# When GpSimd multiplies in a routing head: products tied to VectorE's three lists, and the low parts of down tiles moved behind them

## The reference

```
q = (xt @ w_query).reshape(T, 8, 2, 128)                     # 8 retrieval heads, 2 halves
s = einsum('thpd,hpnd->thpn', q, sub_keys)                   # 128 keys per half
top_s, top_i = top_k(s, 16)                                  # two lists of 16 per head
cand = top_s[:, :, 0, :, None] + top_s[:, :, 1, None, :]
best_s, best_c = top_k(cand, 16)                             # third list
i1, i2 = take_along_axis(top_i[..0], best_c // 16), take_along_axis(top_i[..1], best_c % 16)
ids = i1 * 128 + i2;  gates = softmax(best_s)
a = einsum('tkd,td->tk', expert_down[ids], x)                # 128 experts of 16384 per token
y = einsum('tk,tkd->td', gelu(a) * gates, expert_up[ids])
```

## Time and profile before

| what | us |
|---|---|
| median of three runs | 1589.13 |
| the profiled execution, and its span | 1590.72, 1588.6 |
| head 0 of routing (264.84 to 309.93) | 45.09 |
| heads 1 to 6 (309.93 to 532.80) | 222.87 |
| head 7 and tail (532.80 to 600) | 67.2 |
| TensorE busy over the span | 1487.9 (94%) |
| VectorE, ScalarE, GpSimd busy | 1198.0, 624.7, 591.5 |
| granted TensorE clock, mean | 0.986 |

### The profile page before, as it was taken

The page is one execution under the profiler, slowest core; times in us unless marked ns, Lnnn a source line. Parts: engine busy times, 40 slices in busy tenths (PEclk is TensorE's granted clock), DMA queues, the critical chain, the costliest instruction groups (busy, mean ns, idle before and its releaser), DMA issues.

```text
span 1588.6 us, 21566 instructions
## 1 busy us (share of the span) xinstructions
PE 1487.9 (94%) x7670; PEld 1280.3 (81%) x7670; DVE 1198.0 (75%) x2406; ACT 624.7 (39%) x984; POOL 591.5 (37%) x459
## 2 busy tenths in 40 slices
PE   3999997999999889999968999999999999999997
PEld 3575545998888779999967888888888888888886
DVE  6546435778999987888815887887877887888887
ACT  1114324343344446667713333333343333333333
POOL 0000011225555436999921333334424343443340
PEclk9999998999999999999989999999999999999999
DMA  9962300446444345899987999999989999999993
GB/s 332 361 227 107 107 26 15 144 158 212 158 163 158 118 141 189 243 259 275 283 252 261 343 338 352 350 337 355 341 313 358 346 348 364 339 345 365 342 326 145
DMA packets 258442, 404.90 MB, mean 255 GB/s; under 512 B 120664, under 2 KB 175520, under 8 KB 258208
## 3 DMA queue, kind: packets, MB, share of 16 engines
q1 hardware_dynamic: 122496, 243.87, 43.7%
q0 software_dynamic: 36864, 134.23, 23.5%
q10 hardware_dynamic: 98976, 25.43, 6.9%
HBM read 360.49 MB, written 42.99 MB: 254 GB/s over the span
## 4 chain that ended last, share of the span: by engine, by line
PE 56%; DVE 13%; POOL 5%; issue 5%; ACT 2%; DMA 1%; ACTq 1%; SPq 0%; POOLq 0%; DVEq 0%
PE bank L1695 10%; PE bank L1696 10%; PE bank L1697 10%; PE bank L1639 7%; PE bank L1641 7%; PE bank L1640 7%; POOL gated L672 4%; PE bank L1677 2%; DVE dlo L1204 2%; DVE cand L1248 2%; DMA down<-in_down_t 1%; DVE topi L1194 1%; DVE top L1191 1%; ACTq L916 1%; DVE pick L1232 1%
## 5 line engine op out<-in xcount | busy, mean ns | idle before, releaser
L1639 PE MATMUL bank<-h2hi,dhi 128*128 128x384 f32 x1024 | 351.8, 344 | 45.5 <-DVE dlo L1204 44.2
L1641 PE MATMUL bank<-h2hi,dlo 128*128 128x384 f32 x1024 | 346.3, 338 | 0.0
L1640 PE MATMUL bank<-h2lo,dhi 128*128 128x384 f32 x1024 | 346.0, 338 | 0.0
L1204 DVE TENSOR_TENSOR dlo<-down,dhi 128x1024 fp32r<-128x1024 f32 x128 | 168.0, 1314 | 191.2 <-ACT dhi L820 191.1
L1695 PE MATMUL bank<-uhi,ahi 128*128 128x512 f32 x768 | 300.0, 391 | 4.6 <-DVE ulo L1373 4.6
L1696 PE MATMUL bank<-ulo,ahi 128*128 128x512 f32 x768 | 300.0, 391 | 0.0
L1697 PE MATMUL bank<-uhi,alo 128*128 128x512 f32 x768 | 299.6, 390 | 0.0
L639 POOL DMA_INDIRECT rows<-in_peer_down,ids x128 | 155.3, 1213 | 266.8 <-DVE rows L1217 223.0
L639 POOL DMA_INDIRECT rows<-in_peer_up,ids x128 | 159.6, 1246 | 246.2 <-DVE y L1226 221.3
L1639 PEld LDWEIGHTS bank<-h2hi,dhi 128*128 128x128 f32 x1024 | 194.9, 190 | 54.8 <-DVE dlo L1204 50.7
L1640 PEld LDWEIGHTS bank<-h2lo,dhi 128*128 128x128 f32 x1024 | 195.2, 191 | 2.7
(11 more groups left out here) (198 smaller groups left out, 2030.6 us busy)
## 6 DMA issues: line engine op xcount, KB each, us to landing
down<-in_down_t SPq DMA_DIRECT2D x128, 512.0 KB
up<-in_peer_up SPq DMA_DIRECT2D x128, 512.0 KB
ada<-in_w_ada SPq DMA_DIRECT2D x12, 2048.0 KB, 16.2
gate<-gates_dram SPq DMA_DIRECT2D x128, 192.0 KB
gates_dram<-stage ACTq DMA_DIRECT2D x5, 4096.0 KB, 28.8
gel_dram<-gel SPq DMA_DIRECT2D x80, 192.0 KB
gelu<-gel_dram SPq DMA_DIRECT2D x80, 192.0 KB
wq<-in_peer_query SPq DMA_DIRECT2D x16, 512.0 KB, 4.6
```

The lines of the kernel that those rows point to most:

```text
L1204: ve.tensor_tensor(dlo[s][:], down[s][:], dhi[s][:].bitcast(F32), ALU.subtract).then_inc(dve_dlo, 1)
L1639: pe.matmul(bank[7 * s][:, 0:TD], dhi[s][:, k, :], h2hi[:, k, 0:TD], start=k == 0, stop=False)
L1640: pe.matmul(bank[7 * s][:, 0:TD], dhi[s][:, k, :], h2lo[:, k, 0:TD], start=False, stop=False)
L1641: last = pe.matmul(bank[7 * s][:, 0:TD], dlo[s][:, k, :], h2hi[:, k, 0:TD], start=False, stop=k == KT - 1)
```

## The change

GpSimd's work in a head gets a new order and new waits. For head h (1 to 7) it now waits, by the count of low parts (`dve_dlo`), until VectorE stands at the start of the first list of head h. There it makes `split_wq(h+1, 0)` and the first multiplication of `weigh_hits(h-2)`. It waits until VectorE is past the low part behind the first list, and makes the second multiplication and `split_wq(h+1, 1)`. It waits until the sums of head h are written (`dve_half`), and makes `measure_hits(h-1)`. The gathers come after that.

VectorE's low parts leave the middle of the lists (but for the last head) and stand behind each list. The one ahead of the sums moves ahead of `select`. A fifth stands behind the dots, and head 0 makes one more, so that VectorE is one tile further ahead at the start of each head. The dots in heads fall from 15 to 12 (heads 3 to 6, none in head 7), and `DOTS_ROUTING` from 18 to 15, so the last 3 dots are taken in the main stage.

```diff
-DOTS_ROUTING = DOTS_HEAD * (PH - FIRST_DOTS) + DOTS_PICKS
+DOTS_ROUTING = DOTS_HEAD * (PH - 1 - FIRST_DOTS) + DOTS_PICKS
+def lows_by_head(h):
+    return IN_FRONT + 1 + PER_HEAD * (h + 1)
 # GpSimd
     def measure_hits(h):
+                if h + 2 < PH:
+                    gp.wait_ge(dve_half, h + 2)
...
-            def weigh_hits(h):
+            def weigh_hits(h, s):
+                gp.wait_ge(act_hit, 2 * h + s + 1)
                 gp.wait_ge(dve_top, h + 1)
...
-            for h in range(PH):
-                if h >= FIRST_DOTS - 1:
-                    gathers(min(DOTS_HEAD * (h + 1 - FIRST_DOTS) + ROWS_KEPT + ROWS_HEADS, DOTS_ROUTING))
-                measure_hits(h)
-                weigh_hits(h)
+            for h in range(1, PH):
+                for s in range(2):
+                    if s == 0 or h + 1 < PH:
+                        gp.wait_ge(dve_dlo, lows_by_head(h - 1) + s)
+                    if h + 1 < PH and s == 0:
+                        split_wq(h + 1, 0)
+                    if h >= 2:
+                        weigh_hits(h - 2, s)
+                    if h + 1 < PH and s == 1:
+                        split_wq(h + 1, 1)
+                measure_hits(h - 1)
+                if h >= 2:
+                    gathers(min(DOTS_HEAD * max(h - FIRST_DOTS, 0) + ROWS_KEPT + ROWS_HEADS, DOTS_ROUTING))
+            for s in range(2):
+                weigh_hits(PH - 2, s)
+            measure_hits(PH - 1)
+            gathers(DOTS_ROUTING)
+            for s in range(2):
+                weigh_hits(PH - 1, s)
             gathers(DOTS_ROUTING + ROWS_KEPT)
 # VectorE
-                    top16(lambda b: score[s][:, b, :], lambda b: top[:, s, b, :], lambda b: topi[:, s, b, :], next_lo)
-                    if last:
-                        next_lo()
+                    top16(lambda b: score[s][:, b, :], lambda b: top[:, s, b, :], lambda b: topi[:, s, b, :],
+                          next_lo if last and s else no_lo)
+                    next_lo()
                     if h >= 2 and s == 1 - last:
                         select(h - 2)
                         expert_numbers(h - 2)
-                if last:
-                    sums(h, next_lo)
-                else:
-                    next_lo()
-                    sums(h, lambda: None)
+                sums(h, next_lo if last else no_lo)
...
                 picks_of(h)
-                next_lo()
-                if h >= FIRST_DOTS:
+                if not last:
+                    next_lo()
+                if FIRST_DOTS <= h < PH - 1:
                     for n in range(DOTS_HEAD * (h - FIRST_DOTS), DOTS_HEAD * (h + 1 - FIRST_DOTS)):
                         row_op(n)
+                next_lo()
+                if h == 0:
+                    next_lo()
```

More of the change, by code:

```diff
@@ L643, in _ @@
                     split_wq(h, s)
-            split_wq(2, 0)
             asked = 0
@@ L1204, in down_lo, with no_lo @@
                 ve.tensor_tensor(dlo[s][:], down[s][:], dhi[s][:].bitcast(F32), ALU.subtract).then_inc(dve_dlo, 1)
-            lows = iter(range(FIRST_G))
+            next_low = 0
             def next_lo():
-                n = next(lows)
-                down_lo(n, n % 2)
+                nonlocal next_low
+                down_lo(next_low, next_low % 2)
+                next_low += 1
+            def no_lo():
+                pass
             def row_op(n):
@@ L1340, in _ @@
                 next_lo()
-            assert next(lows, None) is None
+            assert next_low == FIRST_G
             down_lo(FIRST_G, 0)
```

14 lines of the change are left out of this document (5 added, 9 removed).

## The result

| what | before | after | change | forecast |
|---|---|---|---|---|
| median (us) | 1587.44, four runs | 1560.93 (1559.59 to 1561.73), four runs | ratio 0.9833, interval 0.9808 to 0.9859 | 1569, range 1561 to 1583 |
| profiled execution, its span | 1590.72, 1588.6 | 1561.73, 1559.9 | -29.0, -28.7 | 1570.7 |
| head 1 (between first MAX8s) | 34.37 | 33.80 | -0.57 | 0 |
| heads 2 to 6 | 188.50 | 170.65 | -17.85 | -16.6 |
| head 7 and tail, to the first gate product | 77.5 | 72.5 | -5.0 | -3.4 |

The start and the end of the program give the other 0.4. The kernel became faster by 1.7%, where the forecast was 1.3%.

The account below looks back on a forecast made before the run. VectorE, slowed 9.1 us a head by operations colliding with GpSimd products, was taken to hold heads 2 to 6 above TensorE's floor; 1590.7 - 16.6 (heads) - 3.4 (tail) = 1570.7 profiled, so 1569 us median, range 1561 to 1583.

Parts of the forecast that it names:

- The premise: Heads: VectorE's list operations are free beside GpSimd products; MAX8 takes 0.66 and 0.86 against 0.87 us with none running.
- the sum of 9.1 us a head: Head 4, VectorE: cast, sums, low part and list's cast lengthened beside GpSimd products by 1.70 + 3.96 + 1.28 + 2.18.
- Heads 2 to 6: Routing heads: TensorE becomes the bound and each head falls to head 1's 34.37 us, a gain of 16.6 us.
- the other end of the bound: Heads 2 to 6: the floor of head 1's busy time, 34.08 us a head, a gain of 18.1 us.
- The tail: Behind head 7: three dots leave, so the subtraction and the row of steps hanging on it come 3.4 us earlier.
- The dots' term: Tail: without three dots the subtraction ends at 574.8 in place of 578.2, 3.4 us earlier.
- nothing else arrives late enough: Tail: no other step was expected to take back the 3.4 us; `weigh_hits(7)` moves along on the ScalarE queue.
- The sum: Whole kernel: 1590.7 - 16.6 - 3.4 = 1570.7 us for the profiled execution, 1569 us for the median.
- Rival 4: Main stage: the DMA engines decide, and the three moved gathers cost 4.5 us, giving 1574 us; chance 0.08.
- (1): Heads: GpSimd batches slip and collisions stay, heads at 37.3 to 37.7 us, total near 1586 us; chance 0.10.
- (2): Heads: tile D's late transfer holds the chain; at 4 us late the gain falls by 10, giving 1579; chance 0.12.
- Rival 3: Heads: list operations naming two operands lock against GpSimd too, 41.9 us a head, 1607 us in all; chance 0.03.

Follow-up runs that it names:

- The two single halves: Kernel before with GpSimd's new order and waits alone, 1570.37 us; changed kernel with GpSimd's old order, keeping VectorE's new order and 12 dots, 1583.73 us.
- before_again: The kernel before run once more with a profile and no edit; 1587.82 us.
- e2_vector_alone: Changed kernel with GpSimd's old order and waits, keeping VectorE's new order and 12 dots in heads; 1583.73 us.
- e5_offsets_free: Changed kernel without the one wait of GpSimd's offsets on the sums (`dve_half`); 1555.48 us.
- e11_gathers_spread: Changed kernel with the seven gathers of head 2 divided, four in head 2 and three in head 3; 1562.46 us.

## Why the prediction was right in kind and short in size

- **The collisions.** The premise held, and the sum of 9.1 us a head nearly so: VectorE's busy time in head 4 fell by 8.4, from 36.55 to 28.10. The two single halves show that GpSimd's place alone decides it.
- **Heads 2 to 6.** Forecast 16.6, measured 17.85. The price of a head was taken from head 1 as it ran, 34.37, but 0.57 of that was itself VectorE's old order. Its busy time, 34.08, was the other end of the bound and the better one. Head 1 got this 0.57 as well, where the prediction had nothing. The 188.50 that the price was taken from also holds 1.5 us of TensorE's clock, in head 2 (0.96), which the prediction's rows show as 0.99 over all five heads and which it didn't name. With the waits gone the clock stayed at 1.00, so this part came back too.
- **The tail.** Forecast 3.4, measured 5.0. The dots' term was right: 3.5. The other 1.5 is a transfer. Behind `select(7)` the kernel before has one that ScalarE waits for, and the one after doesn't. ScalarE before:

```profile
596.62 1.06 ACT L820 ACTIVATE dhi<-down 128x1024 fp32r<-128x1024 f32 x1 [1.43 <-DMA down<-in_down_t]
```

  It was issued at 590.51, beside a gather, and took 6.1 us. The same tile's after was issued at 567.97 with no gather near, and was there when ScalarE came to it:

```profile
572.85 1.05 ACT L834 ACTIVATE dhi<-down 128x1024 fp32r<-128x1024 f32 x1
```

  With GpSimd's order alone this wait is gone too, and the tail is 1.5 shorter than before: 76.0. In `before_again` it is 0.84, and the tail lies between, at 77.0. The prediction put nothing for it ("nothing else arrives late enough"). That the gather made it late was not tried.
- **The turns.** This is the step that failed, and the largest: 4.6 us. The sum "1590.7 - 16.6 - 3.4" has no term for this stage, and the prediction read no row of it, because the change doesn't touch it. GpSimd bounds it in part, and by how much varies: 186.2 and 188.5 in two runs of the kernel before, 183.9 and 181.5 in two of the one after. With one product fewer on GpSimd it is 181.5 in both. So no work was saved here. Whether the change makes the long pairs rarer, or the 4.6 us are luck of two profiled executions, these runs don't settle: the other kernels with GpSimd's changed order and the pair took 181.5 to 186.3, and `e2_vector_alone`, with its old order, 182.7. What is known is that the prediction put this stage at nothing because its code is the same, while its length moved by 2.3 and 2.4 us with no edit at all. The other 3.4 us of the 8 are the terms for heads and tail, each too small.
- **The main stage.** Three more dots and gathers cost 0.8 and -0.1 in two runs, against a bound of 4.5. Rival 4 is out.
- **Rivals 1 to 3.** Collisions did not stay in heads 1 to 6 (1), though in the tail a cast of 1.87, sums of 2.80 and a subtraction of 2.42 did. D's low part waited 0.21 for its high part (2); what came late was another transfer, of the next head's tile B, by up to 0.7 us of TensorE. And the lists don't lock (3): a MAX8 group takes 0.86 or 0.87 beside products and without. In the first two lists of heads 1 to 6 of the changed kernel 70 of 96 FIND_INDEX8 and 41 of 48 MATCH_REPLACE8 lie beside a product. Their medians are 0.288 and 0.278 us, and 0.285 and 0.276 for those beside none. Rival 3 rested on their naming two operands. The rows show two instructions, each with one input (first the 8 values, then the 128 scores):

```profile
413.43 0.07 DVE L1208 MATCH_VALUE_LOAD topi<-top,score 128x8 f32 x1
413.49 0.28 DVE L1208 FIND_INDEX8 topi<-top,score 128x8 uint32<-128x128 f32 x1
```

  The Trainium skill (SBUF — State Buffer, section "SBUF: two separate sides") gives the exclusive lock to VectorE operations in a two-port mode or with two SBUF inputs. The sums and low parts, with two inputs, and the casts, with one, behave like that here. The list operations, with one input each, do not, and that goes with the page too.
- **The sum.** Against 1570.7, the profiled execution was 9.0 lower: turns 4.6, heads 1.8, tail 1.6, the small stretches 0.7, and 0.3 outside the span. The range's lower end had room for the heads' part (1.5 us below) and for a fast run, but none for the tail or for a stage that no row was read of. That the median lies 0.07 us outside, and not inside, says little, as the turns alone differ by 2.4 between runs of one kernel; the terms that were too small would be so either way.

## To carry to other kernels

Here a cast, a sum or a low part that started beside a GpSimd product lasted until that product ended (0.17 became 1.87), and list operations did not, so order GpSimd by what VectorE does beside it. Look first at where VectorE has slack: in `e5_offsets_free` two collisions a head cost nothing. Low parts moved behind a long block need one more tile ahead, or TensorE pays for the move (2.1 us a head here). Read rows of the stages that an edit leaves alone as well: the turns differed by 2.3 and 2.4 us between runs of one kernel, against a term of 3.4 for the tail. And read the granted clock by head before a difference of 1.5 us is put down to the order of the work.

## What the runs showed that was not expected

- GpSimd's pair of gated products beside VectorE's runs in 1.70 or in 2.4 to 4.7 us with the same instructions, and stays in one way for several turns.
- A wait of TensorE can cost more than its length, through the granted clock. The same wait of 2.7 us late in a head of the old order was followed by a fall in some heads, which then last 1.5 or 2.8 us longer, and by none in others. In the tail, the kernel with GpSimd's order alone (a wait of 6.00 us) and the changed one (2.56), in the 14 us that hold this wait:

```profile
560.00:574.00 14.00, 8.00 (x36) 7.64 (x35) 10.01 (x12) 8.86 (x10) 5.03 (x2) 0.76 0.29 86
```

```profile
557.00:571.00 14.00, 8.69 (x49) 8.05 (x48) 10.96 (x8) 9.54 (x11) 5.17 (x2) 1.00 0.50 156
```

The first is a mean of 2.4 GHz and of the lower level, 1.2 GHz; the second is 2.4 GHz throughout. The clock fell at the wait of 6.00 in all five runs that have it. At the one of 2.56 to 2.58 it stayed up in both runs of the changed kernel and fell in others with the same tail: in `e11_gathers_spread` the 14 us from 559 have a clock of 0.88. So the length of the wait alone doesn't decide it, and what does stays open.
